# Score tiles of latent attention: groups of three instead of pairs

## What is computed

```python
s = (einsum('bqhd,bshd->bhqs', qn_b, k_nope)
     + einsum('bqhr,bsr->bhqs', qr_b, k_r)) * scale      # scale = 96 ** -0.5
p = softmax(s, axis=-1)                                  # over all S keys, no mask
o = einsum('bhqs,bshd->bqhd', p, v)                      # 8 heads, 64 values each
```

## Time and profile before

| | us |
|---|---|
| runs shown: lowest, median, highest (2 runs) | 6909.74, 6985.69, 7061.65 |
| the profiled execution | 6650.5 |
| its span, slowest core (core 5) | 6649.0 |
| span of the eight cores | 6614.4 to 6649.0 |
| TensorE busy in the span | 5287.1 (80%) |
| ScalarE busy in the span | 3693.0 (56%) |
| VectorE busy in the span | 1590.7 (24%) |

### The profile page before, as it was taken

One profiled execution on the slowest core, in us unless ns is written; L12 is line 12 of the kernel. 1 busy time (PEld: TensorE's weight loads), 2 busy tenths in 40 slices (PEclk: granted clock), 3 DMA queues, 4 the chain that ended last, 5 costly groups with the idle time before them and its releaser, 6 DMA issues.

```text
span 6649.0 us, 80984 instructions; the slowest of 8 cores (6614.4 to 6649.0 us)
## 1 busy us (share of the span) xinstructions
PE 5287.1 (80%) x24082; PEld 2077.8 (31%) x24082; DVE 1590.7 (24%) x2463; ACT 3693.0 (56%) x5317; POOL 40.1 (1%) x73
## 2 busy tenths in 40 slices
PE   2554688878895666656989889898988978888888
PEld 1221233323342222223333333333333333333333
DVE  2332333321212333323121221212122112111111
ACT  2434577752222455565979779797987952222221
POOL 0000000000000000000000000000000000000000
PEclk8665799989997677657999999999999989999999
DMA  4444000014452000021000000000000024444444
GB/s 129 133 147 136 22 1 1 1 57 141 139 153 93 25 25 23 23 66 44 1 1 1 1 1 1 1 1 1 1 1 1 1 75 141 141 141 136 139 138 144
DMA packets 264375, 403.61 MB, mean 61 GB/s; under 512 B 88466, under 2 KB 157458, under 8 KB 261266
## 3 DMA queue, kind: packets, MB, share of 16 engines
q1 hardware_dynamic: 257042, 373.27, 18.8%
q0 software_dynamic: 6912, 25.17, 1.0%
HBM read 349.51 MB, written 48.82 MB: 60 GB/s over the span
## 4 chain that ended last, share of the span: by engine, by line
PE 67%; ACT 10%; DMA 8%; DVE 7%; issue 6%; SPq 1%; ACTq 0%; DVEq 0%; POOLq 0%
PE ps L800 17%; PE ps L784 16%; PE ps L932 7%; PE ps L938 7%; PE ps L968 6%; PE ps L464 4%; ACT arena L790 3%; PE ps L870 2%; DMA arena<-s_wd 2%; PE ps L600 1%; ACT arena L418 1%; PE ps L708 1%; ACT arena L596 1%; DMA arena<-w_down 1%; DMA arena<-ropeR_s 1%
## 5 line engine op out<-in xcount | busy, mean ns | idle before, releaser
L790 ACT ACTIVATE arena<-ps 128x1024 bf16<-128x1024 f32 x2560 | 2361.0, 1171 | 172.4 <-PE ps L784 172.1
L784 PE MATMUL ps<-arena 96*128 96x512 bf16 x5120 | 1523.9, 385 | 132.3 <-DVE arena L770 132.3
L800 PE MATMUL ps<-arena 128*128 128x512 bf16 x5120 | 1531.2, 380 | 101.3 <-ACT arena L790 101.3
L807 DVE RECIPROCAL arena<-ps 64x512 f32<-64x512 f32 x96 | 322.5, 3359 | 2178.0 <-PE ps L800 2178.0
L784 PEld LDWEIGHTS ps<-arena 96*128 96x128 bf16 x5120 | 500.5, 98 | 767.8 <-issue 174.7
L800 PEld LDWEIGHTS ps<-arena 128*128 128x128 bf16 x5120 | 345.8, 96 | 1024.3 <-issue 1001.7
L932 PE MATMUL ps<-arena 128*128 128x512 bf16 x2112 | 516.9, 389 | 113.7 <-DMA arena<-s_wg 106.0
L968 PE MATMUL ps<-arena 128*128 128x512 bf16 x2112 | 483.8, 385 | 68.4 <-DVE arena L974 32.8
L944 ACT ACTIVATE arena<-ps 128x512 f32<-128x512 f32 x264 | 156.6, 594 | 655.1 <-PE ps L932 647.6
L938 PE MATMUL ps<-arena 128*128 128x512 bf16 x2112 | 504.1, 382 | 4.2 <-DVE arena L946 4.1
L464 PE MATMUL ps<-arena 128*128 128x512 bf16 (+2 forms) x1552 | 445.1, 462 | 2.7 <-ACT arena L458 2.7
(11 more groups left out here) (99 smaller groups left out, 3354.6 us busy)
## 6 DMA issues: line engine op xcount, KB each, us to landing
arena<-s_wg SPq DMA_DIRECT2D x264, 256.0 KB, 2.7
arena<-s_wu SPq DMA_DIRECT2D x264, 256.0 KB, 2.7
arena<-s_wd SPq DMA_DIRECT2D x528, 128.0 KB, 2.2
arena<-xp SPq DMA_DIRECT2D x96, 512.0 KB, 3.6
arena<-xs SPq DMA_DIRECT2D x48, 512.0 KB, 3.9
yp<-arena POOLq DMA_DIRECT2D x32, 512.0 KB, 4.0
arena<-w_gate SPq DMA_DIRECT2D x8, 1408.0 KB, 8.5
arena<-w_up SPq DMA_DIRECT2D x8, 1408.0 KB, 8.2
```

The source lines that it names most:

```text
L784: ins = e.matmul(bank(b0 + u)[:, 0:QB], lhsT=KT[0:96, kt * 128:(kt + 1) * 128], rhs=QT[0:96, qs], start=True, stop=True)
L790: P.op("act", lambda e: e.activation(out=pt_.rearrange("p (a b) -> p a b", a=2)[:, :, 0:QB], in_=src, func=AF.Exp, scale=SC_B), reads=[ban ...
L800: ins = e.matmul(bank(ob)[:, 0:QB], lhsT=Vh[:, kt, :], rhs=pt_[:, u * 512:u * 512 + QB], start=(kt == 0), stop=(kt == nt - 1))
L807: P.op("dve", lambda e: e.reciprocal(out=osb[0:64, :], in_=bank(ob)[64:128, 0:QB]), reads=[bankres[ob]], writes=[r_osb])
```

## The change

The pairs become groups of three tiles, with what is left over in one or two groups of two. For 64 tiles `gsz` is twenty threes and two twos (22 groups in place of 32 pairs); for 32 tiles it is ten threes and one two (11 groups in place of 16 pairs). A group takes three banks, so the six score banks hold two groups, `b0 = (g % 2) * 3`. One exponential covers up to 1536 columns, and each of the three `PT` buffers grows from 1024 to 1536 elements. The order of the list changes too: `qk(0)`, `qk(1)`, the epilogue of the block before, then for each group `pv(g)` followed by `qk(g + 2)`. Before, `qk` of a pair stood ahead of the `pv` of the pair two behind it.

```diff
-            PT = A.alloc("PT", [1024], BF16, slots=3)
+            PT = A.alloc("PT", [1536], BF16, slots=3)
...
-                npair = nt // 2
+                g3, rem = nt // 3, nt % 3
+                if rem == 0:
+                    gsz = [3] * g3
+                elif rem == 2:
+                    gsz = [3] * g3 + [2]
+                else:
+                    gsz = [3] * (g3 - 1) + [2, 2]
+                gst = [sum(gsz[:i]) for i in range(len(gsz))]
+                ng = len(gsz)
...
-                    def qk(p, qs=qs):
-                        b0 = (p % 3) * 2
+                    def qk(g, qs=qs):
+                        b0 = (g % 2) * 3
+                        sz, k0 = gsz[g], gst[g]
 
                         def f(e):
-                            for u in range(2):
-                                kt = 2 * p + u
+                            for u in range(sz):
+                                kt = k0 + u
                                 ins = e.matmul(bank(b0 + u)[:, 0:QB], lhsT=KT[0:96, kt * 128:(kt + 1) * 128],
                                                rhs=QT[0:96, qs], start=True, stop=True)
                             return ins
-                        P.op("pe", f, reads=[r_KT, r_KTr, r_QT], writes=[bankres[b0], bankres[b0 + 1]])
...
+                        P.op("pe", f, reads=[r_KT, r_KTr, r_QT], writes=[bankres[b0 + u] for u in range(sz)])
+                        (pt_, rpt) = PT[g % 3]
+                        src = ps_t[:, b0 * 512:(b0 + sz) * 512].rearrange("p (a b) -> p a b", a=sz)[:, :, 0:QB]
+                        P.op("act", lambda e: e.activation(
+                            out=pt_.rearrange("p (a b) -> p a b", a=3)[:, 0:sz, 0:QB],
+                            in_=src, func=AF.Exp, scale=SC_B),
+                            reads=[bankres[b0 + u] for u in range(sz)], writes=[rpt])
...
-                    for p in range(npair):
-                        qk(p)
-                        if p == 2 and pend:
-                            pend.pop()()
-                        if p >= 2:
-                            pv(p - 2)
-                    pv(npair - 2)
-                    pv(npair - 1)
+                    qk(0)
+                    qk(1)
+                    if pend:
+                        pend.pop()()
+                    for g in range(ng):
+                        pv(g)
+                        if g + 2 < ng:
+                            qk(g + 2)
                     pend.append(epilogue)
```

More of the change, by code:

```diff
@@ L786, in f, with pv @@
                             return ins
-                        P.op("pe", f, reads=[r_KT, r_KTr, r_QT], writes=[bankres[b0], bankres[b0 + 1]])
[L788 to L795, removed]
+                        P.op("pe", f, reads=[r_KT, r_KTr, r_QT], writes=[bankres[b0 + u] for u in range(sz)])
[5 more added lines that the diff above has]
+                            reads=[bankres[b0 + u] for u in range(sz)], writes=[rpt])
+                    def pv(g, ob=ob):
+                        (pt_, rpt) = PT[g % 3]
+                        sz, k0 = gsz[g], gst[g]
                         def f(e):
-                            for u in range(2):
-                                kt = 2 * p + u
+                            for u in range(sz):
+                                kt = k0 + u
                                 ins = e.matmul(bank(ob)[:, 0:QB], lhsT=Vh[:, kt, :],
```

## The result

The changed kernel took 7080.97 us (median of 11 runs, 7063.6 to 7401.52); the kernel before, with the runs made beside it, 6783.86 us (median of 10, 6647.06 to 7061.65). The ratio is 1.0641, 95% interval 1.0622 to 1.0659: slower. The profiled execution after took 7078.72 us (core 6 is the slowest, span 7077.2), 428.2 more than before.

What follows compares the result with a forecast made beforehand. The loop exponential, pv, qk between ScalarE and TensorE was taken to become the bound: 6650.5 us profiled + 454 (prompt 367, sample 87) + 280 of carried-over excess = 7385 us, with an 8-in-10 range of 7060 to 7500.

Steps and rivals of the forecast that it cites:

- The ring: MLA stages: exponential, pv, qk, next exponential into the same banks outlasts both engines' work; +454 us, chance with excess 0.63.
- turn: One pass round the loop of exponential, pv and qk in the MLA blocks: 3.27 us for two groups.
- TensorE's wait: In the MLA blocks, pv waits for ScalarE's exponential, about 0.33 us per group on average.
- ScalarE's gap: In the MLA blocks, ScalarE idles before exponentials, 0.28 us per group on average, alternating between about none and 0.56.
- forecast releasers: In the MLA blocks, L784 ends ScalarE's gaps of some 0.28 us; ScalarE ends pv's wait of about 0.33.
- the handover: From an exponential's end to its pv: 0.26 us kept from a bare block start; 0.15 at a block's end gives +356.
- What was costed at nothing: MLA stages: same 10240 matmuls, moved epilogue, three PT buffers; first block of each head 0, within 16 us.
- Batching's own gain: MLA stages: 800 fewer exponentials at 0.06 us fixed part could spare 48 us, worth nothing under the longer loop.
- The clock: Rival: TensorE's stops in each group lower its clock to 1.2 GHz half the time; +1257 us, 7908 us, chance 0.04.
- the likeliest case: The exchange loop bounds the MLA stages and the shown runs' excess carries over: 7266 to 7543 us, chance 0.63.
- the carry-over of 280 us of excess: Whole kernel: of the 335 us by which the shown runs' median exceeds the profiled time, 280 are added.
- The rival without excess: Whole kernel: the exchange loop holds but the shown runs' excess is absent; 7105 us, +6.8% on the profiled time, chance 0.23.

Runs made afterwards that it cites:

- qk first: The changed kernel with qk(g + 2) written ahead of pv(g) within a block; ratio to the kernel before 0.9974.
- two buffers: The kernel before, still in pairs, with two score buffers and the changed kernel's order, pv(p) then qk(p + 2); ratio 1.0955.
- 0.69 (three): The kernel before with its three score buffers kept and only the order changed to pv(p), then qk(p + 2); 7211.05 and 7212.38 us, about 1.085.

## Why the prediction was right, and where it was off

**The ring was the bound.** Undoing it alone (qk first) brought 1.064 back to 0.997; making it without wide exponentials cost more (1.0955); shortening it by one matmul shortened each turn by that matmul. TensorE's wait and ScalarE's gap stood where they were forecast, with the forecast releasers, and the MLA stages took 2656 and 802 us where 2690 and 810 were forecast. The gaps are smaller than forecast, 0.41 and 0.40 us per turn, 0.20 per group, in place of 0.28 and 0.33.

**Its size.** 454 us were forecast and 428 measured. The turn was 3.20, not 3.27: two errors against each other. The leg from the exponential to `pv` is 1.59 to 1.60, not 1.71. The exponential of 1536 columns takes 1.45 (an exponential record's mean is 1448 ns), as worked out; the handover was 0.15, as in the earlier trace rows, not the 0.26 of a block's start that I kept. The argument for keeping it (TensorE waiting in both) picked the wrong row. The leg from `qk` to the exponential is 0.96 to 0.97, not 0.91. With both, a prompt block is 35.77 in place of 36.45 and a sample block 18.47 in place of 18.75, 53 us less for all blocks. What was costed at nothing gives 27 of them back: the head changes are 6 us longer in the prompt (80.0 to 80.7 between epilogues against 73 to 75) and 3 in the sample, because the new head's first block, which they hold, is longer by the ring as every block is, and by about 1 us more; the rest is in the blocks that take 0.28 more and in what lies outside the MLA stages. So 428 lies nearer to 454 than the turn alone would have it, and that is luck.

**Batching's own gain.** 48 us were forecast as what 800 fewer exponentials could spare, and worth nothing under the ring. The changed kernel loses it in the gaps, and it comes out as 0.67 us per prompt block where neither ring nor edge is in the way. In the time of a whole kernel even there no more than 9 to 43 us of it were seen (6517.48 us against 6526.88 to 6560.21).

**The clock.** The granted clock stayed at 1.00, the level of 2.4 GHz, in the blocks with an idle 0.40 us in each turn of 3.20. The Trainium skill (TensorE: Matmul & The Clock Gate, section "A second HAM failure mode: psum-queue depth-cycling") tells of a kernel in which short idles between groups of matmuls that cycle through PSUM banks made the clock go back and forth. This trace has such idles in every turn and does not agree.

**The time itself.** The point, 7385 us, was 304 over the median of 7081, and the likeliest case, with 0.63, began at 7266. The step that failed is the carry-over of 280 us of excess: I took the runs shown for what the kernel does, while five later runs of it took 6647 to 6658 us, like the profiled execution, and three 6962 to 7000. No clock is on record for the two runs shown, so that what made them long is not shown. The rival without excess, 7105 us, is what came true, within 0.4%. It had 0.23, and deserved the larger part: no row of the trace shows the excess, and the same program had shown that it could run without it. The measured 7081 lies 21 us above the lower end of the range of 7060 to 7500, which reaches so far down for this rival's sake alone; the ring was forecast, but that the range holds the time is in part luck.

## What to carry to other kernels

Before making the pieces of a double-buffered exchange between two engines larger at the cost of their number, add up the ring from bare handovers in the trace (here 1.60 + 0.65 + 0.96 us) and compare it with the number of buffers times the slower engine's piece. If it is longer, first look at what stands ahead of the refill in the feeding engine's list: the consumer's `pv` had no need to be there, and moving it took the ratio from 1.064 to 0.997. The gaps at the edges of the loop were worth more (1.2 to 1.7% of the time) than the fixed cost that larger pieces save: 0.67 us of 29.33 per block, and at most 0.6% of the whole time.

## What was not expected of the hardware

Where a bank had been released just ahead of its refill, the exponential came 0.05 to 0.06 us later behind its `qk` than where the bank had long been free: 0.75 (two buffers) against 0.69 (three) for two tiles, 0.96 in the changed kernel's turn against 0.91 at its block's start (4895.65 to 4896.56) for three. The matmuls themselves started 0.216 us apart in both. That the release is what delays it is a guess; no run took it apart.

The third bank of an exponential costs what its 512 columns cost elsewhere, and nothing for being a third bank: 1.02 and 1.45 us alone, 0.917 and 1.344 us as a pace, so 0.43 for it in both, as between one bank and two.
